# A fused two-block kernel: the first, banded and differential stages in another order, and the rotary cosine products on GpSimd

## The reference

```
mod = silu(c) @ w_ada + b_ada                       # 1024 x 3072: shift, scale, gate
h = rms_norm(x, g_pre) * (1 + scale) + shift
qa, ka, va, fa, za, qb, kb, vb, zb = split(h @ w_in)
oa = forgetting_attention(qa, ka, va, fa + b) * silu(za)      # 8 heads of 64, causal
qb, kb = rope(qb), rope(kb)                                   # x1 cos - x2 sin, x2 cos + x1 sin
ob = sliding_window_sink_attention(qb, kb, vb, sinks) * silu(zb)   # 8 heads, window 128
x = x + gate * rms_norm([oa, ob] @ w_out, g_post)

# block 2: three branches that share h = rms_norm(x)
differential attention: for each of 8 heads two maps m = 0, 1 of head size 64,
    q, k = rms_norm(q), rms_norm(k)
    p_m = softmax(q_m k_m / 8 - slope * distance, causal);  o = (p_0 - lam p_1) v
    o = rms_norm(o) * silu(gate)
convolution branch (31 taps), memory cross attention (256 rows of mem_2, 4 heads)
x = x + (merge gates * the three projections) @ w_out
```

## Time and profile before

| what | value |
|---|---|
| median of 3 runs | 1310.44 us (1307.08 to 1310.52) |
| the profiled execution: its time, its span | 1308.47 us, 1306.7 us |
| mean PE clock granted, share of full speed | 0.981 |
| PE busy | 1231.2 us (94%), 6554 matmuls |
| DVE busy | 862.7 us (66%) |
| ACT busy | 595.3 us (46%) |
| POOL busy | 60.6 us (5%) |
| DMA | 130.11 MB, mean 100 GB/s |

### The profile page before, as it was taken

One profiled execution on the slowest core, in us unless ns is written; L12 is line 12 of the kernel. 1 busy time (PEld: TensorE's weight loads), 2 busy tenths in 40 slices (PEclk: granted clock), 3 DMA queues, 4 the chain that ended last, 5 costly groups with the idle time before them and its releaser, 6 DMA issues. The chain is left out here.

```text
span 1306.7 us, 17243 instructions
## 1 busy us (share of the span) xinstructions
PE 1231.2 (94%) x6554; PEld 1019.7 (78%) x6554; DVE 862.7 (66%) x1425; ACT 595.3 (46%) x1090; POOL 60.6 (5%) x60
## 2 busy tenths in 40 slices
PE   5988899997789999999999998999999899999998
PEld 4888788786579997777777776788888688788888
DVE  4786766756667424788778877488777578773341
ACT  5544354443446445555555655332555312652220
POOL 2009300000000000000000000000000000000001
PEclk9989999998899999999999999999999999999999
DMA  9876221210145421221222114223221333332321
GB/s 330 288 243 218 74 66 55 65 44 6 33 147 173 158 73 64 81 69 40 70 65 81 65 33 145 81 97 98 81 71 59 113 97 98 92 102 90 99 71 49
DMA packets 34227, 130.11 MB, mean 100 GB/s; under 512 B 3969, under 2 KB 4225, under 8 KB 33633
## 3 DMA queue, kind: packets, MB, share of 16 engines
q1 hardware_dynamic: 30672, 111.69, 26.4%
q0 software_dynamic: 3184, 17.01, 3.6%
q10 hardware_dynamic: 288, 0.31, 0.1%
HBM read 122.70 MB, written 6.29 MB: 99 GB/s over the span
## 5 line engine op out<-in xcount | busy, mean ns | idle before, releaser
L415 PE MATMUL bank<-hl,wh 128*128 128x512 f32 x880 | 368.2, 418 | 7.4 <-ACT th L1013 4.7
L417 PE MATMUL bank<-hh,wh 128*128 128x512 f32 x880 | 346.3, 394 | 0.0
L416 PE MATMUL bank<-hh,wl 128*128 128x512 f32 x880 | 345.8, 393 | 0.0
L985 ACT ACTIVATE wh<-raw 128x1024 fp32r<-128x1024 f32 x187 | 192.3, 1054 | 217.5 <-PE bank L417 193.2
L1581 DVE TENSOR_TENSOR wl<-raw,wh 128x1024 fp32r<-128x1024 f32 x187 | 227.0, 1238 | 79.8 <-ACT wh L985 78.2
L415 PEld LDWEIGHTS bank<-hl,wh 128*128 128x128 f32 x880 | 167.1, 190 | 48.9 <-issue 13.8
L416 PEld LDWEIGHTS bank<-hh,wl 128*128 128x128 f32 x880 | 167.6, 190 | 36.5 <-issue 6.5
L417 PEld LDWEIGHTS bank<-hh,wh 128*128 128x128 f32 x880 | 166.8, 190 | 37.1
L1975 DVE SCALAR_TENSOR_TENSOR ca<-u,vt,ca 128x512 f32<-128x512 f32 x232 | 157.9, 744 | 0.0
L415 PE MATMUL bank<-wl,hh 128*128 128x256 f32 (+1 forms) x352 | 102.6, 291 | 6.5 <-DVE cumt L1668 3.4
L416 PE MATMUL bank<-wh,hl 128*128 128x256 f32 (+1 forms) x352 | 100.5, 286 | 0.0
(11 more groups left out here) (304 smaller groups left out, 1976.1 us busy)
## 6 DMA issues: line engine op xcount, KB each, us to landing
raw<-in_chunks SPq DMA_DIRECT2D x211, 512.0 KB, 4.0
x<-in_x POOLq DMA_DIRECT2D x4, 512.0 KB, 10.8
mem_scratch<-kvm POOLq DMA_DIRECT2D x1, 2048.0 KB, 6.8
x<-in_x POOLq DMA_DIRECT2D x1, 2048.0 KB, 8.5
x_scratch<-x POOLq DMA_DIRECT2D x1, 2048.0 KB, 6.5
kvm<-mem_scratch POOLq DMA_DIRECT2D x1, 2048.0 KB, 8.2
x1r<-x_scratch POOLq DMA_DIRECT2D x1, 2048.0 KB, 8.5
out_x<-x1r POOLq DMA_DIRECT2D x8, 256.0 KB, 2.5
```

The lines of the kernel that those rows point to most:

```text
L415: pe.matmul(o, a[0], b[1], start=start, stop=False, **kw)
L416: pe.matmul(o, a[1], b[0], start=False, stop=False, **kw)
L417: return pe.matmul(o, a[0], b[0], start=False, stop=stop, **kw)
L985: act.activation(wh[:, SLOT[nxt]], raw[:, NRAW[nxt] % RAWS], ACT.Copy).then_inc(s.w_hi, 1)
```

## The change

It joins three reorderings and a move of work.

1. **First stage.** Sixteen of the 24 `w_ada` pieces go to eight slots of their own (in the space of `hh` and `hl`, which are free until h is written), the others through `raw`; the order of loads is a new table. `mod` is taken at g = 2. ACT loads the square root's table first and takes the tanh of c after the memory's root. The first memory chunk waits for its parts one by one. Some small steps of DVE stand earlier.
2. **Banded stage.** Scores use two banks in place of three, the rotation gets bank 4. A unit's bank is opened by one 512-wide mask matmul. From n = 34 on PE does the pieces (all but one), values, turn, rotation, the last piece and then scores; DVE's gated output, query split and gate stand between row maxima and normalising.
3. **Rotation.** DVE keeps the sine's product; GpSimd does the cosine's product and the addition.
4. **Differential stage.** Score operands are 128 rows high, with zeros in the other map's rows of the queries (`qz`) and keys of both maps in `kd`. DVE and ACT split a head in three steps in place of two. `diff_turn` stands right behind the scores for tt < 3 and two pieces later for tt = 3. The sums of squares are taken at tt = 1 and 2, ACT scales them out of PSUM (`mean_of`) and takes one logarithm and one exponential over all three rows at tt = 2. The gate `dg` is taken at tt = 3 in place of the next head's tt = 0.

```diff
-ROTATE = {27: ("kb", 0), 29: ("qb", 0), 35: ("qb", 1), 38: ("qb", 2), 42: ("qb", 3)}
-EVEN = {7: 1, 15: 2, 23: 3, 30: 4, 36: 5, 39: 6, 43: 7}
+ROTATE = {27: ("kb", 0), 29: ("qb", 0), 34: ("qb", 1), 38: ("qb", 2), 42: ("qb", 3)}
+EVEN = {7: 1, 15: 2, 23: 3, 30: 4, 35: 5, 39: 6, 43: 7}
...
+ADA_SLOTS, ADA_EARLY = 8, 16
+ADA_BEHIND = (0, 2, 1, 2, 1, 1, 1, 1, 1, 1, 1, 1, 2, 1, 0, 0, 0, 2, 0, 2, 0, 2, 0, 2)
 RAW = []
-for _i in range(12):
-    RAW = RAW + CHUNKS[2 * _i:2 * _i + 2] + [("ada", 2 * _i + j) for j in range(2)]
+for _i, _n in enumerate(ADA_BEHIND):
+    RAW = RAW + [CHUNKS[_i]] + [("ada", sum(ADA_BEHIND[:_i]) + j) for j in range(_n)]
...
+RAW_SLOT, RAW_BEFORE, _held, _at = {}, {}, {}, 0
+for _name in RAW:
+    if _name[0] == "ada" and _name[1] < ADA_EARLY:
+        _slot = RAWS + _name[1] % ADA_SLOTS
+    else:
+        _slot, _at = _at % RAWS, _at + 1
+    RAW_SLOT[_name], RAW_BEFORE[_name] = _slot, _held.get(_slot)
...
-                if g == 3:
-                    pe.wait_ge(s.ada_used, 16)
+                if g == 2:
+                    pe.wait_ge(s.ada_used, ADA_EARLY)
...
-                b = 2 + u_ % 3
+                b = 2 + u_ % 2
...
+                    pe.matmul(ps[b][:], ident_b[:], wmask[:].rearrange("p a n -> p (a n)"), start=True, stop=True)
+                    if pair == 0:
+                        pe.matmul(ps[b][:, 0:P], ident_b[:], masks[:, 1, :], start=False, stop=True, skip_group_check=True)
                     for i in range(2):
                         tt = 2 * pair + i
                         q_ = slice(tt * P, tt * P + P)
-                        lo, at = max(tt - 1, 0) * P, 256 * i
-                        if tt == 0:
-                            pe.matmul(ps[b][:, 0:P], ident_b[:], masks[:, 0, :], start=True, stop=False)
-                            pe.matmul(ps[b][:, 0:P], ident_b[:], masks[:, 1, :], start=False, stop=True)
-                            at = P
+                        lo, at = max(tt - 1, 0) * P, 256 * i + (P if tt == 0 else 0)
                         w = 256 * (i + 1) - at
-                        o = ps[b][:, at:at + w]
-                        three(o, (qz[:, hh_ % 2, 0, q_], qz[:, hh_ % 2, 1, q_]), (kp0[:, 0, lo:lo + w], kp0[:, 1, lo:lo + w]),
-                              True, False)
-                        ins = pe.matmul(o, ident_b[:], masks[:, 2 - w // P:2, :], start=False, stop=True)
+                        for n, (q, k) in enumerate(((0, 1), (1, 0), (0, 0))):
+                            ins = pe.matmul(ps[b][:, at:at + w], qz[:, hh_ % 2, q, q_], kp0[:, k, lo:lo + w], start=False,
+                                            stop=True, skip_group_check=True)
                 banks.close(ins, ("S", u_))
 
             def turn(u_, key, src_blocks, b=6):
...
-                banks.open(pe, 7, ("rot",) + key)
-                banks.close(pe.matmul(ps[7][:], rot[:], qf[:, 0, :], start=True, stop=True), ("rot",) + key)
+                banks.open(pe, 4, ("rot",) + key)
+                banks.close(pe.matmul(ps[4][:], rot[:], qf[:, 0, :], start=True, stop=True), ("rot",) + key)
...
+                unit_scores(n)
+            for n in range(FOX + 2, UNITS + 3):
                 if n < UNITS:
+                    done = FILLED[n - 1]
+                    pieces(FILL, done, FILLED[n] - done - 1)
+                else:
+                    wo_part((n - UNITS) // 2, (n - UNITS) % 2, range(0, C - 1))
+                if n >= FOX + 4 and n % 2 == 0:
+                    values_window((n - FOX - 4) // 2)
+                if n < UNITS + 2:
+                    unit_turn(n - 2)
+                if n in ROTATE:
+                    rotate(ROTATE[n])
+                if n < UNITS:
+                    pieces(FILL, FILLED[n] - 1, 1)
                     unit_scores(n)
-            for i in range(2):
...
+                    pe.wait_ge(s.q_lo, Q1 + 3 * j + 3)
+                outs = [ps[2 + 2 * (u_ % 2) + m][:, 0:w] for m in range(2)]
                 for m in range(2):
-                    b = 2 + 2 * (u_ % 2) + m
-                    half = slice(HD * m, HD * m + HD)
-                    banks.open(pe, b, ("D", u_, m))
-                    o = ps[b][:, 0:w]
-                    three(o, (qh[half, q_], ql[half, q_]), (kh[half, 0:w], kl[half, 0:w]), True, False)
-                    pe.matmul(o, slopes[:, j, :], dist[:, S - w:S], start=False, stop=True)
-                    ins = pe.matmul(ps[b][:, w - P:w], ident_b[:], masks[:, 1, :], start=False, stop=True,
+                    banks.open(pe, 2 + 2 * (u_ % 2) + m, ("D", u_, m))
+                    three(outs[m], (qz[:, m, 0, q_], qz[:, m, 1, q_]), (kd[:, j % 2, 0, 0:w], kd[:, j % 2, 1, 0:w]), True, False)
+                for m in range(2):
+                    pe.matmul(outs[m], slopes[:, j, :], dist[:, S - w:S], start=False, stop=True)
+                for m in range(2):
+                    ins = pe.matmul(outs[m][:, w - P:w], ident_b[:], masks[:, 1, :], start=False, stop=True,
                                     skip_group_check=True)
...
+                    pieces(fill, at, half)
                     diff_scores(j, tt)
+                    if tt in (1, 2) and j < 7:
+                        pe.wait_ge(s.squared, 4 + 2 + 2 * j + tt)
+                        total(("dns", 2 * j + 1 + tt), [norms[:, tt - 1, :]], blocks)
+                    if tt < 3 and 4 * j + tt > 0:
+                        diff_turn(4 * j + tt - 1)
                     pieces(fill, at + half, 2)
+                    if tt == 3:
+                        diff_turn(4 * j + tt - 1)
                     if tt == 1 and j > 0:
                         diff_values(j - 1)
                     pieces(fill, at + half + 2, half - 2)
                     if tt == 1 and j > 0:
                         subln(j - 1)
-                    if 4 * j + tt > 0:
-                        diff_turn(4 * j + tt - 1)
             pieces([("md", 0)], 0, 5)
             diff_turn(31)
...
+            pool.wait_ge(s.rope_out, 2)
+            for n in sorted(ROTATE):
+                key, turn = ROTATE[n], sorted(ROTATE).index(n)
+                banks.wait_empty(pool, key)
+                pool.wait_ge(s.q_lo, SPLITS_DONE[n])
+                pool.tensor_tensor(qf[:, 1, :], qf[:, 0, :], cos[:], ALU.mult).then_inc(s.rope_cos, 1)
+                pool.wait_ge(s.rope_cos, turn + 1)
+                banks.wait_empty(pool, ("rot",) + key)
+                pool.tensor_tensor(qf[:, 1, :], qf[:, 1, :], rs, ALU.add).then_inc(s.roped, 1)
+                pool.wait_ge(s.roped, turn + 1)
...
+            def mean_of(key, dst, n):
+
+                banks.wait_full(act, key)
+                banks.empty(act.activation(dst, ps[7][:], ACT.Identity, scale=1.0 / n, bias=eps6), key)
+
+            def roots_together(keys, rows):
+
+                for key in keys:
+                    banks.wait_empty(act, key)
+                logs[0] += 1
+                act.activation(rows, rows, ACT.Ln).then_inc(s.logged, 1)
+                act.wait_ge(s.logged, logs[0])
+                act.activation(rows, rows, ACT.Exp, scale=-0.5).then_inc(s.rms_done, 1)
+                rms[0] += 1
+                for key in keys:
+                    roots[key] = rms[0]
...
-            act.activation(warm, eps6, ACT.Tanh)
-            act.wait_ge(s.rows_in, 16)
-            act.activation(tc_, v8("c"), ACT.Tanh, scale=0.5).then_inc(s.c_tanh, 1)
-            act.activation(warm2, eps6, ACT.Sqrt)
+            act.activation(warm, eps6, ACT.Sqrt)
             act.wait_ge(s.mem_in, 16 * 2)
             square_rows(memx, MEM_SS, 2)
             act.wait_ge(s.sumsq, 2)
             act.activation(MEM_SS, MEM_SS, ACT.Sqrt, scale=1.0 / D, bias=eps6).then_inc(s.small_sqrt, 1)
+            act.wait_ge(s.rows_in, 16)
+            act.activation(tc_, v8("c"), ACT.Tanh, scale=0.5).then_inc(s.c_tanh, 1)
...
+            def split_head(j, last_scores):
+
+                act.activation(kd[:, j % 2, 0, :], qf[:, 1, :], ACT.Copy).then_inc(s.q_hi, 1)
+                banks.wait_full(act, last_scores)
+                for m in range(2):
+                    half = slice(HD * m, HD * m + HD)
+                    act.activation(qz[half, m, 0, :], qf[half, 0, :], ACT.Copy).then_inc(s.q_hi, 1)
...
+            def rope_sin(key, turn):
+
+                banks.wait_full(dve, ("rot",) + key)
                 dve.wait_ge(s.rope_out, 2)
-                then(dve.tensor_tensor(qf[:, 1, :], qf[:, 0, :], cos[:], ALU.mult))
-                banks.wait_full(dve, ("rot",) + key)
-                banks.empty(dve.tensor_tensor(rs, ps[7][:], sin[:], ALU.mult), ("rot",) + key)
```

259 lines of the change are left out of this document (146 added, 113 removed).

## The result

Before 1309.18 us, changed 1288.56 us (medians of 4 runs each, 1286.6 to 1288.95 for the changed one): a ratio of 0.9841, 95% interval 0.9822 to 0.986. The kernel is 20.6 us faster, where 39 was forecast, and the median lies 0.6 us above the range's upper end. The profiled execution has a span of 1286.9 us.

A forecast was written before the change was run, and what follows sets the result against it. PE, busy 94% of the span, was taken as the bound, so gains come from its waits, lower clock or own work. First stage -12, banded -17, differential -10: 1308.5 - 39 = 1269.5, forecast 1270 us, range 1254 to 1288.

The forecast's parts named there:

- Step (a): Start of the first stage: the square root's table is loaded before the memory arrives, gaining 2.2 us (1.4 to 2.5).
- Step (b): First stage: the first memory chunk no longer waits for all parts; the 2.1 us wait falls to 0.3, gaining 1.8.
- Step (c): First stage: the 3.3 us wait for `macc` goes, since sixteen `w_ada` pieces no longer queue for four slots.
- Step (d): First stage: the 15.35 us stretch at clock 0.67 behind the `macc` wait goes, gaining 5.1 us.
- Step (e): First stage: `mod` comes earlier, so DVE has longer for h; 1.6 of the logarithms' 3.4 us wait is gained.
- 4.6 us a unit: Banded stage: each of 14 units takes 4.6 us in place of 5.85, a gain of 17.4 us.
- The wait for the turn, 0.9 a head: Differential stage: PE waits 0.5 to 1.2 us for `prob` at tile 3's turn; 0.9 in seven heads costs 6.3.
- The differential gain is lost: Rival, 1280 us: row height isn't the cost, or PE waits at the turn for its gain; chance 0.20.
- DVE and GpSimd bound the banded stage: Rival, 1278 us: DVE takes 5.2 us a banded unit in place of 4.6, giving back 8.4; chance 0.09.
- No wait for the turn: Rival, 1263 us: DVE reaches tile 3's probabilities in 18.1 us or less, so PE doesn't wait; chance 0.15.
- the loads hide the first stage: Rival, 1278 us: transfers leave no room, so only 4 of the first stage's 12 us stay; chance 0.04.
- slower: Rival, 1318 us: tile 3's turn waits for the whole chain, 7.9 us in each of seven heads; chance 0.05.

The follow-up runs named there:

- e14: Changed kernel with ACT's first steps in the old order (table and tanh of c, then the square root's table): 1288.64 us.
- e11: Changed kernel with the banded stage's splits of turned probabilities ahead of exponentials and normalising, as before the change: 1283.26 us.
- e8: Changed kernel with the cosine's product and the addition of the rotation back on DVE: 1288.36 us.
- e7: Kernel before, with both maps' 64-row differential score products next to each other and the distances behind them: 1298.73 us.
- e13: e9 with the score products padded to 128 rows, nothing else: 1270.62 us.
- e9: Changed kernel with tile 3's turn two pieces later, gate behind split, 64-row products, and tile 3's split ahead of two weights: 1268.59 us.
- e4: Changed kernel with DVE's gate behind the split of tile 2's turned probabilities: 1278.59 us.
- e1: Changed kernel with the turn of tile 3 back behind all pieces of the next head's tile 0: 1278.77 us.
- e10: Changed kernel with PE's values behind a unit's scores in the banded stage: 1299.04 us.
- e2: e1 with 64-row score products in the differential stage: 1278.3 us.

## Why the prediction was wrong

- **First stage, -12:** measured -11.8, and most of its parts are near too. Step (a), 2.2 us for the start, measured 2.6 at PE's first matmul (14.1 to 11.5), but e14 shows that it reaches the end of the stage with 0.9 at most and the whole time with nothing that can be seen. Step (b), 1.8, was 1.7. Step (c) happened: the wait for `macc` is gone. Step (d), 5.1, came only in part: no stretch like the one of 15 us at clock 0.67 is left, but a new one of 6.8 us at the lower level stands at the waits for `norms` and `wl`, so that all lower clock up to the stage's end fell by 3.4 us. Step (e), 1.6 for the logarithms, was 2.4. Those two waits are 4.5 us where two for `wl`, 2.3 in all, stood before: 2.2 more, the cost that I had put at 2.
- **Banded stage, -17:** measured -10.3, 0.7 outside its range (-11 to -24). The term that failed is "4.6 us a unit". It was 5.13. I had said that gated output, split and gate would fill DVE's wait for ACT, and had not looked at what left that place: the split of turned probabilities. Of 10.5 us that DVE waited, 9.6 stayed, and PE's values waited 10.2 for that split in five places. The 4.6 also took for granted a full clock, of which no step of the change made sure: it was 0.92 before and 0.90 after, 7 us of the window. With a clock of 0.98 the same order takes 4.89 a unit (e14), and with the split back in place, at full clock, 4.74 (e11). So about half of the miss of 0.53 goes with the clock and a part of the rest with the split.
- **Rotation on GpSimd:** priced at 2.6 to 4.4 us for a pair on POOL, hidden; measured 2.55 to 2.9, hidden, worth nothing (e8). What failed is the 4.1 us taken off DVE's work: DVE got 0.4 of them. The Trainium skill's rule ("SBUF — State Buffer", "SBUF: two separate sides": a shared pair of ports, held exclusively) agrees with the rows: a DVE operation of 0.23 us lasts 0.82 and ends with POOL's.
- **Differential stage, -10:** measured +2.4, outside its range (-17 to -3). Two steps. The term "2.2 us less PE work a head" was good: PE's busy time in a head fell from 41.3 to 38.8, 2.5. Its cause was half right. The time at a switch of row height is there, but the order alone gives nearly as much (e7: 2.3 us less work with 64 rows), since 64-row products of the two maps run at the same time. The prediction had set a rule of the Trainium skill ("TensorE: Matmul & The Clock Gate", "Why this matters for your kernels") against its rows: what gains is to run small matmuls side by side. On the padding this rule was right: e13 against e9 shows 0.65 us a head of PE work lost by it, 0.3 of it in the time of a head.
- **The wait for the turn, 0.9 a head,** is the step that broke the forecast. I took `prob` of tile 3 as "what is late next", and its time was within what I had allowed: 18.6 to 19.3 us behind the maxima of tile 2, 19.27 measured, since the roots came 2.0 us earlier and not 3.3. PE arrives 18.0 us behind the maxima, as counted, so `prob` alone would have cost 1.2. But the turn opens bank 6, and that is emptied by DVE's split of the turn before, which stands behind the probabilities and the gate: 1.1 us more. Five waits of 2.45 and one of 3.1 are 15.4 in place of 6.3: 9 us. The lower clock at the waits, which I named among what would make the prediction wrong but left out of the sum, is 1.3 to 1.6 us for each of five heads, some 7. e4 shows the queue on DVE to be the cause of the wait, and with shorter or moved waits the five slow stretches became three (e4), one (e1) and none (e9).
- **The rivals.** "The differential gain is lost" (1280) was nearest in kind, in its second form: PE waits at the turn for what it gained. "DVE and GpSimd bound the banded stage" had a unit right by luck (5.2, measured 5.13): not GpSimd, which e8 clears, but the split's place and the clock made it so. The prediction let one rival at a time come true, but both losses fell on this kernel: 1269.5 with 10 and 8.4 given back is 1287.9, near the measured 1288.56 and at the very end of the range. "No wait for the turn", "the loads hide the first stage" and "slower" didn't happen.

What stays open: why e10's order lets turn and split wait for each other, why a wait of 2.45 us goes with a slow stretch in some heads and not in others (the window from 546.35 has none), and how much of the banded stage's 5.13 us a unit the clock alone would give back.

## What to carry to other kernels

When an instruction is moved ahead on PE, look at each of its waits, the one for its output's bank too, and read on the engine that frees this bank what is queued ahead of the freeing instruction. When steps are swapped on an engine, ask what the step that leaves was covering: here a split of 0.6 us had filled a wait for ACT in each unit. And when waits move from place to place at the same length of a period (40.1 to 40.6 us in five runs, in heads without a slow stretch), look for the loop and cut its last step, as e9 does.

## What the runs showed of the hardware

Two fp32 matmuls of 64 rows, one on rows 0 to 63 and one on rows 64 to 127, start 0.01 us apart and end together when nothing of 128 rows stands between the products of the two maps. The widest unit takes 1.43 us then (e2), 1.93 with products of 128 rows (e1), and 2.41 with 64 rows and a 128-row matmul between the maps (the kernel before). The program lists three products of map 0 and then three of map 1, and the trace of e2 has them in pairs: first with first, second with second, third with third.

A VectorE operation beside a two-operand one on GpSimd can be held back until that one ends: 0.82 us in place of 0.23, and 0.83 to 0.85 in place of 0.16, four times in the changed kernel's banded units.
